# First tile of a token mixer: its input projection taken row block by row block, with the loads put in another order

## The chip, the cores and the metric

The kernel runs on one core of one Trainium2 chip. The metric is device time in microseconds (us) of that core; lower is better. Before the change, three runs took 5826.6, 5829.93 and 5834.68 us (median 5829.93).

## The reference, cut to what matters

Two transformer blocks follow one another on 2048 tokens of width 1024. The change lies in the opening of the first block, in its mixer:

```
hn   = rms_norm(x, norm_mix_w)            # x: 2048 x 1024
proj = hn @ w_in                          # w_in: 1024 x 2560 -> q, k, v, g, u (512 columns each)
q, k = rope(q, positions), rope(k, positions)
ret  = silu(g) * retention(q, k, v, ret_gn_w)
pool = pool_mixer(u, pool_w, pool_scale)
h    = x + concat([ret, pool]) @ w_out    # w_out: 1024 x 1024
```

After that come the router and 32 experts, a gated side branch, and the second block (latent attention, a bidirectional state-space layer, an output projection). None of these is touched.

## The kernel before, in words

The program is a row of phases, each of which waits for the one before. The first, `mixer_phase`, walks over 16 tiles of 128 tokens. Each engine has its own program, written out by hand in the order in which it runs, and engines meet at semaphores (`then_inc` and `wait_ge`); nothing reorders this. TensorE's program for a tile is `body` (L653): it transposes the x of the next tile, projects the next tile's five blocks of 512 columns between the steps of the present tile, and ends with the router's logits. `project(t, n)` (L630 to L638) makes one block of 512 columns: eight matmuls, one for each block of 128 rows of `w_in`, summed in one bank of PSUM, `PJ0` or `PJ1` in turn. ScalarE copies a bank out (`evacuate`, L319), times the row's 1/rms.

The first tile has no tile before it, so what it needs is made ahead of the loop, and this is where the change is:

- SyncE issues the loads in this order (L229 to L245): five small vectors and the broadcast `gain_moe` with `pos_i` (the positions) last, x of tile 0, zeros for the list of tokens `tok_list`, the eight row blocks of `w_in` (1280 KB each), the router's and pool's weights, eight row blocks of `w_out`, x of tile 1.
- ScalarE multiplies each row block of `w_in` in place by its gain (`scale_w_in`, L374): four blocks, then the tables (sin, cos, decays, L387 to L393), then the other four. Only the last block raises `w_in_scaled` (L397).
- VectorE makes angles and window matrices (L413 to L433, which ends with `dve_setup`), then, when `w_out` has landed, multiplies it by its gain (L551), and only then starts the rotation of tile 0 (L477).
- TensorE transposes x of tile 0 (L627), waits for `w_in_scaled`, makes the five projections one after another, 40 matmuls, waits for `dve_setup` to reach 2 (the scaled `w_out`), and goes into `body(0)`.
- GpSimd zeroes half of `xT` first (`zero_i`, L271), the source of the zeros that are stored to `tok_list`; ScalarE may overwrite `xT` only when that store has landed (L379).

Of the kernel before, what the change touches and what calls it, by code (L numbers as in the profile page):

```python
# [38 lines left out]
E, TOPK, CAP = 32, 4, SEQ  # L39
# [63 lines left out]
def mixer_phase(nc, I, S):  # L103
# [3 lines left out]
    with ExitStack() as ctx:  # L107
# [26 lines left out]
        pos_i = sb("pos_i", [P, TILES], I32)  # L134
# [9 lines left out]
        xT = sb("xT", [P, KD, P])  # L144
# [27 lines left out]
        zero_i = xT[:, 0:4, :].rearrange("p k c -> p (k c)").bitcast(I32)  # L172
# [30 lines left out]
        KV = pb("KV", BANK)  # L203
        Y = pb("Y", BANK)

        names = [f"w_in_rows{k}" for k in range(KD)] + """loads weights w_in_scaled pool_chain dve_setup act_setup pool_setup tables_in sines
# [18 lines left out]
        def _(sp):  # L225
            def load_x(t, par):
                sp.dma_start(x_sb[:, par, :], x_t[bass.ds(t, 1)].squeeze(0)).then_inc(s["x_loaded"], 16)

            sp.dma_start(gain_mix[:, :], I["norm_mix_w"][0].rearrange("(k p) -> p k", p=P)).then_inc(s["loads"], 16)  # L229
# [4 lines left out]
            sp.dma_start(pos_i[:, :], I["positions"][0].rearrange("(t p) -> p t", p=P)).then_inc(s["loads"], 16)  # L234
            load_x(0, 0)
            sp.wait_ge(s["pool_setup"], 1)
            sp.dma_start(S["tok_list"].rearrange("(p n) o -> p (n o)", p=P), zero_i[:, :]).then_inc(s["list_zeroed"], 16)
            for k in range(KD):
                sp.dma_start(w_in[:, k, :], I["w_in"][0, k * P:(k + 1) * P, :]).then_inc(s[f"w_in_rows{k}"], 16)
# [5 lines left out]
            load_x(1, 1)  # L245

# [22 lines left out]
        def _(pool):  # L269
            ch = Chain(pool, s["pool_chain"])  # L270
            ch.link(pool.memset(zero_i, 0))  # L271
            pool.sem_inc(s["pool_setup"], 1)
# [36 lines left out]
        def _(act):  # L309
# [9 lines left out]
            def evacuate(t, par, n, has_prev):  # L319
                act.wait_ge(s["proj_ps"], t * 5 + (n + 1))  # L320
                if n == 0:
                    act.wait_ge(s["rstd1_ready"], t + 1)
                if n == 4 and has_prev:
                    act.wait_ge(s["pl_ps"], t)
                if n < 2:
                    dst = qk[:, n * HEADS:(n + 1) * HEADS, :, :].rearrange("p h two f -> p (h two f)")
                else:
                    dst = vgu[:, par, (n - 2) * BANK:(n - 1) * BANK]
                act.activation(dst, PJ[n % 2][:, :], ACT.Copy, scale=rstd1[:, :]).then_inc(s["proj_sb"], 1)
# [44 lines left out]
            def scale_w_in(k):  # L374
                act.wait_ge(s[f"w_in_rows{k}"], 16)
                return act.activation(w_in[:, k, :], w_in[:, k, :], ACT.Copy, scale=gain_mix[:, k:k + 1])  # L376

            norm_x(0, 0)
            act.wait_ge(s["list_zeroed"], 16)  # L379
            copy_xT(0)  # L380

            act.wait_ge(s["loads"], 16 * 6)
            for k in range(4):
                scale_w_in(k)
            act.wait_ge(s["pool_setup"], 2)
# [9 lines left out]
            for k in range(4, KD):  # L395
                last = scale_w_in(k)
            last.then_inc(s["w_in_scaled"], 1)  # L397
            for n in range(5):
                evacuate(0, 0, n, False)
# [8 lines left out]
        def _(dve):  # L408
            ch = Chain(dve, s["dve_chain"])
            dve.wait_ge(s["pool_setup"], 2)  # L410
            dve.wait_ge(s["loads"], 16 * 6)
# [58 lines left out]
            def body(t, par, has_prev, has_next):  # L470
# [15 lines left out]
                if has_next:  # L486
                    norm_x(t + 1, True)
                dve.wait_ge(s["qkT_sb"], t + 1)
# [57 lines left out]

            norm_x(0, False)

            dve.wait_ge(s["weights"], 16 * (KD + 2))
            for k in range(KD):  # L550
                last = dve.tensor_scalar(w_out[:, k, :], w_out[:, k, :], gain_out[:, k:k + 1], None, ALU.mult)  # L551
            last.then_inc(s["dve_setup"], 1)
# [66 lines left out]
        def _(pe):  # L619
            pe.wait_ge(s["pool_setup"], 2)  # L620
# [32 lines left out]
            def body(t, par, has_prev, has_next):  # L653
# [58 lines left out]
                pe.wait_ge(s["mx_sb"], t + 1)  # L712
                project_out(0, range(4, KD))
# [22 lines left out]
            pe.wait_ge(s["w_in_scaled"], 1)  # L736
            for n in range(5):
                project(0, n, False)
            pe.wait_ge(s["dve_setup"], 2)
# [2283 lines left out]
```

## Time and profile before

| | us |
|---|---|
| median of three runs | 5829.93 (5826.6 to 5834.68) |
| the profiled execution | 5826.38 |
| its span, first to last instruction | 5824.6 |
| TensorE busy | 5316.9 (91%) |
| VectorE busy | 3248.5 (56%) |
| ScalarE busy | 2129.4 (37%) |
| GpSimd busy | 707.8 (12%) |

The span is what the profiler sees; the time of that execution is 1.8 us more. The mean granted clock of TensorE over the span is 0.962 of full speed. Of 40 slices of 145.6 us, the first has TensorE busy in six tenths; the next six are at nine tenths, and so is most of the rest. The last piece of the first phase ends about 1120 us into the span.

How the rows further on are read. A row of the timeline gives the start, the length, the engine, the line of the kernel, the operation, what it writes `<-` what it reads, the shape, how many records in a row were joined, and in brackets how long the engine had been idle before it and what released it. An fp32 matmul leaves two records (passes), so 40 matmuls are x80. The groups come in the order in which the prediction uses them.

### The profile page before, as it was taken

The page shows a single profiled execution, that of the slowest core. Times are in us where ns is not written, and L with a number is a line of the kernel's source. Part 1 is how long each engine was busy: PE and PEld are TensorE (multiplying, and loading weights), DVE is VectorE, ACT ScalarE, POOL GpSimd, SP SyncE. Part 2 cuts the span into 40 slices and gives each one's busy share as a digit, 9 for nine tenths or more (in the row PEclk, how much of TensorE's full clock was granted, in tenths as well). Part 3 has the DMA queues.
Part 4 walks back from the last instruction along what each step waited for, and adds up shares of the span by engine and source line. Part 5 has one row for each costly group of instructions (what it writes and reads, how often), then busy time and mean ns, then how long its engine had stood idle before and what let it go on. Part 6 is the DMA issues. An engine that isn't in the chain of part 4 may idle for free. (4 is left out here: it accounts for less than half of the span.)

```text
span 5824.6 us, 77622 instructions
## 1 busy us (share of the span) xinstructions
PE 5316.9 (91%) x24587; PEld 3508.7 (60%) x24922; DVE 3248.5 (56%) x6128; ACT 2129.4 (37%) x3190; POOL 707.8 (12%) x901
## 2 busy tenths in 40 slices
PE   6999999499999999999999999599995599999688
PEld 3555555366666666666666666355554477777365
DVE  3433433477676767777777777433335544443277
ACT  3111111144443545555555554222222433333243
POOL 0000000100000000000000000001003399100000
PEclk9999999699999999999999999799997799999899
DMA  3111211356464647777777676422322300000433
GB/s 136 57 50 54 72 50 50 115 176 192 159 207 150 211 152 238 237 237 240 239 232 234 229 227 204 161 93 103 103 89 97 82 5 8 6 6 6 170 108 101
DMA packets 424599, 769.80 MB, mean 132 GB/s; under 512 B 57440, under 2 KB 142368, under 8 KB 422816
## 3 DMA queue, kind: packets, MB, share of 16 engines
q1 hardware_dynamic: 363984, 607.16, 31.5%
q10 hardware_dynamic: 33216, 87.05, 4.9%
q0 software_dynamic: 27280, 74.02, 4.0%
q8 instruction: 73, 1.20, 0.1%
q14 instruction: 46, 0.38, 0.0%
HBM read 628.36 MB, written 139.76 MB: 132 GB/s over the span
## 5 line engine op out<-in xcount | busy, mean ns | idle before, releaser
L1070 DVE TENSOR_TENSOR w_lo<-stage,w_hi 128x1024 bf16<-128x1024 f32 (+1 forms) x800 | 929.6, 1178 | 201.3 <-ACT w_hi L939 142.3
L939 ACT ACTIVATE w_hi<-stage 128x1024 fp32r<-128x1024 f32 (+1 forms) x800 | 791.7, 1017 | 575.9 <-PE GU L773 291.2
L770 PE MATMUL GU<-w_hi,x_hl 128*128 128x512 f32 x2048 | 860.1, 420 | 19.0 <-DVE x_hl L1075 7.6
L771 PE MATMUL GU<-w_hi,x_hl 128*128 128x512 f32 x2048 | 811.6, 396 | 0.0
L636 PE MATMUL PJ<-w_in_sb,xT 128*128 128x512 f32 x1280 | 579.6, 607 | 41.9 <-ACT w_in_sb L376 31.5
L773 PE MATMUL GU<-w_lo,x_bf 128*128 128x512 bf16 x1920 | 480.6, 381 | 7.7
L770 PEld LDWEIGHTS GU<-w_hi,x_hl 128*128 128x128 f32 x2048 | 386.5, 189 | 135.1 <-issue 27.9
L770 PE MATMUL Y<-w_hi,a_hl 128*128 128x512 f32 x1024 | 456.8, 446 | 0.0
L636 PEld LDWEIGHTS PJ<-w_in_sb,xT 128*128 128x128 f32 x1280 | 244.2, 195 | 332.8 <-issue 286.2
L771 PEld LDWEIGHTS GU<-w_hi,x_hl 128*128 128x128 f32 x2048 | 387.5, 189 | 82.9
L771 PE MATMUL Y<-w_hi,a_hl 128*128 128x512 f32 x1024 | 404.4, 395 | 0.0
L773 PEld LDWEIGHTS GU<-w_lo,x_bf 128*128 128x128 bf16 x2048 | 174.7, 98 | 255.4 <-issue 89.8
L2337 DVE TENSOR_REDUCE ntop<-SC 128x1 f32<-128x2048 f32 x64 | 146.7, 2292 | 284.9 <-PE SC L2446 284.9
L900 POOL DMA_INDIRECT rows<-hn,ids x77 | 79.8, 1036 | 1780.4 <-PE TX L1209 1260.4
L2473 PE MATMUL O<-probsT,z_c 128*128 128x128 f32 x2048 | 276.1, 282 | 12.2 <-ACT probsT L2245 12.2
L945 ACT ACTIVATE acted<-pre 128x256 f32<-128x256 f32 (+1 forms) x304 | 131.9, 434 | 412.9 <-DVE pre L1098 399.8
L773 PE MATMUL Y<-w_lo,a_bf 128*128 128x512 bf16 x960 | 273.3, 383 | 4.4
L2473 PEld LDWEIGHTS O<-probsT,z_c 128*128 128x128 f32 x2048 | 248.2, 191 | 29.5 <-ACT probsT L2245 24.0
L1600 PE MATMUL G<-w_gate,hT 128*128 128x512 f32 x512 | 229.7, 608 | 30.4 <-ACT hT L1430 23.8
L1094 DVE TENSOR_TENSOR pre<-GU,b_gu 128x512 f32<-128x512 f32 x256 | 175.4, 685 | 137.1 <-PE GU L773 136.4
L643 PE MATMUL TR<-w_out_sb,catT 128*128 128x512 f32 x512 | 226.3, 595 | 0.7 <-ACT catT L358 0.7
L770 PEld LDWEIGHTS Y<-w_hi,a_hl 128*128 128x128 f32 x1024 | 193.2, 189 | 51.1
(537 smaller groups left out, 8752.2 us busy)
## 6 DMA issues: line engine op xcount, KB each, us to landing
stage<-in_expert_w_gate_up_dram SPq DMA_DIRECT2D x512, 512.0 KB, 5.2
stage<-in_expert_w_down_dram SPq DMA_DIRECT2D x224, 512.0 KB, 6.7
expert_rows<-zero_y SPq DMA_DIRECT2D x16, 2048.0 KB, 10.0
b_gu<-in_expert_b_gate_up_dram ACTq DMA_DIRECT2D x128, 256.0 KB, 4.9
expert_rows<-acted ACTq DMA_DIRECT2D x64, 512.0 KB, 2.9
b_d<-in_expert_b_down_dram ACTq DMA_DIRECT2D x32, 512.0 KB, 8.0
stage<-in_expert_w_down_dram SPq DMA_DIRECT2D x64, 256.0 KB, 3.3
z<-z_sb SPq DMA_DIRECT2D x16, 992.0 KB, 8.1
```

What stands on the lines that cost most here:

```text
L636: mm = pe.matmul(PJ[n % 2][:, :], xT[:, k, :], w_in[:, k, n * BANK:(n + 1) * BANK], start=(k == 0), stop=(k == KD - 1))
L643: mm = pe.matmul(TR[:, n * BANK:(n + 1) * BANK], catT[:, k, :], w_out[:, k, n * BANK:(n + 1) * BANK], start=(k == 4), stop=(k == 3))
L770: pe.matmul(out, high(k), w_high(k), start=(k == first), stop=False)
L771: pe.matmul(out, low(k), w_high(k), start=False, stop=False)
L773: mm = pe.matmul(out, short(k), w_low(k), start=False, stop=(k == last))
L939: act.activation(w_hi[:, c, ks, :], staged, ACT.Copy).then_inc(s["hi_done"], 1)
L945: act.activation(act_of(c)[0:n], gate[0:n], ACT.Tanh, scale=ALPHA / 2).then_inc(s["tanh_ready"], 1)
L1070: dve.tensor_tensor(w_lo[:, c, ks, :], staged, w_hi[:, c, ks, :], ALU.subtract).then_inc(s["lo_done"], 1)
L1094: ch.link(dve.tensor_tensor(pre[:, :], GU[c][:, :], b_gu[:, cols], ALU.add))
L1600: mm = pe.matmul(G[:, n * BANK:(n + 1) * BANK], hT[:, k, :], w_gate[:, k, n * BANK:(n + 1) * BANK], start=(k == 0), stop=(k == KD - 1))
L2337: dve.tensor_reduce(ntop[:, h % 2:h % 2 + 1], SC[:, :], AX, ALU.min).then_inc(s["max_done"], 1)
L2473: mm = pe.matmul(O[:, h * P:(h + 1) * P], c_rows(kt), probsT[:, j, kt % 4 * P:(kt % 4 + 1) * P], start=(kt == 0), stop=(kt == TILES - 1))
```

## The change

- SyncE: x of tile 0 is issued first, then `gain_mix` and `pos_i` (on a semaphore of their own, `gain_in`), then the eight row blocks of `w_in`, and the other small loads after them. The zeros for `tok_list` come last and are read from `zero_y`.
- GpSimd no longer zeroes `xT`; ScalarE no longer waits for that store.
- Each scaled row block of `w_in` raises `w_in_scaled`. For tile 0 TensorE loops over row blocks outside and the five column blocks inside, into five banks at once: `PJ0`, `PJ1`, `KV`, `Y` and the first half of `SC`.
- VectorE scales `w_out` in the body of tile 0, behind the rotation and the norm of tile 1; TensorE waits for it ahead of the first product with `w_out`.

```diff
+        first_banks = [PJ[0], PJ[1], KV, Y, SC]
...
-            sp.dma_start(gain_mix[:, :], I["norm_mix_w"][0].rearrange("(k p) -> p k", p=P)).then_inc(s["loads"], 16)
+            load_x(0, 0)
+            sp.dma_start(gain_mix[:, :], I["norm_mix_w"][0].rearrange("(k p) -> p k", p=P)).then_inc(s["gain_in"], 16)
+            sp.dma_start(pos_i[:, :], I["positions"][0].rearrange("(t p) -> p t", p=P)).then_inc(s["gain_in"], 16)
+            for k in range(KD):
+                sp.dma_start(w_in[:, k, :], I["w_in"][0, k * P:(k + 1) * P, :]).then_inc(s[f"w_in_rows{k}"], 16)
...
-            load_x(0, 0)
-            sp.wait_ge(s["pool_setup"], 1)
-            sp.dma_start(S["tok_list"].rearrange("(p n) o -> p (n o)", p=P), zero_i[:, :]).then_inc(s["list_zeroed"], 16)
-            for k in range(KD):
-                sp.dma_start(w_in[:, k, :], I["w_in"][0, k * P:(k + 1) * P, :]).then_inc(s[f"w_in_rows{k}"], 16)
...
             load_x(1, 1)
+            sp.wait_ge(s["pool_setup"], 1)
+            sp.dma_start(S["tok_list"].rearrange("(p n c) o -> p n (c o)", p=P, c=P),
+                         zero_y[:, :].bitcast(I32).unsqueeze(1).to_broadcast([P, E * CAP // (P * P), P])).then_inc(s["list_zeroed"], 16)
...
-            ch.link(pool.memset(zero_i, 0))
-            pool.sem_inc(s["pool_setup"], 1)
...
-                return act.activation(w_in[:, k, :], w_in[:, k, :], ACT.Copy, scale=gain_mix[:, k:k + 1])
+                act.activation(w_in[:, k, :], w_in[:, k, :], ACT.Copy, scale=gain_mix[:, k:k + 1]).then_inc(s["w_in_scaled"], 1)
...
-            act.wait_ge(s["list_zeroed"], 16)
...
-            act.wait_ge(s["loads"], 16 * 6)
+            act.wait_ge(s["gain_in"], 32)
...
-            dve.wait_ge(s["loads"], 16 * 6)
+            dve.wait_ge(s["gain_in"], 32)
...
+                if not has_prev:
+                    scale_w_out()
                 dve.wait_ge(s["qkT_sb"], t + 1)
...
+            def scale_w_out():
+                dve.wait_ge(s["loads"], 16 * 4)
+                dve.wait_ge(s["weights"], 16 * (KD + 2))
+                for k in range(KD):
+                    last = dve.tensor_scalar(w_out[:, k, :], w_out[:, k, :], gain_out[:, k:k + 1], None, ALU.mult)
+                last.then_inc(s["dve_setup"], 1)
...
                 pe.wait_ge(s["mx_sb"], t + 1)
+                if not has_prev:
+                    pe.wait_ge(s["dve_setup"], 2)
...
-            pe.wait_ge(s["w_in_scaled"], 1)
-            for n in range(5):
-                project(0, n, False)
-            pe.wait_ge(s["dve_setup"], 2)
+            for k in range(KD):
+                pe.wait_ge(s["w_in_scaled"], k + 1)
+                if k % 4 == 0:
+                    pe.wait_ge(s["xT_sb"], k // 4 + 1)
+                for n, bank in enumerate(first_banks):
+                    mm = pe.matmul(bank[:, 0:BANK], xT[:, k, :], w_in[:, k, n * BANK:(n + 1) * BANK],
+                                   start=(k == 0), stop=(k == KD - 1))
+                    if k == KD - 1:
+                        mm.then_inc(s["proj_ps"], 1)
```

TensorE at the opening of the program, before: the transposes of x of tile 0 into `TR`, then the projection of tile 0 into the two `PJ` banks.

```order
L627 MATMUL TR<-ident,x_sb 128x128 [waits x_loaded,pool_setup]
L627 MATMUL TR<-ident,x_sb 128x128 x7
L636 MATMUL PJ<-w_in_sb,xT 128x512 [waits xT_sb,w_in_scaled]
L636 MATMUL PJ<-w_in_sb,xT 128x512 x3
L636 MATMUL PJ<-w_in_sb,xT 128x512 [waits xT_sb]
L636 MATMUL PJ<-w_in_sb,xT 128x512 x11
L636 MATMUL PJ<-w_in_sb,xT 128x512 [waits proj_sb]
L636 MATMUL PJ<-w_in_sb,xT 128x512 x7
```

The same place after the change, with the first two of eight groups.

```order
L628 MATMUL TR<-ident,x_sb 128x128 [waits x_loaded,pool_setup]
L628 MATMUL TR<-ident,x_sb 128x128 x7
L744 MATMUL PJ<-w_in_sb,xT 128x512 [waits xT_sb,w_in_scaled]
L744 MATMUL PJ<-w_in_sb,xT 128x512
L744 MATMUL KV<-w_in_sb,xT 128x512
L744 MATMUL Y<-w_in_sb,xT 128x512
L744 MATMUL SC<-w_in_sb,xT 128x512
L744 MATMUL PJ<-w_in_sb,xT 128x512 [waits w_in_scaled]
L744 MATMUL PJ<-w_in_sb,xT 128x512
L744 MATMUL KV<-w_in_sb,xT 128x512
L744 MATMUL Y<-w_in_sb,xT 128x512
L744 MATMUL SC<-w_in_sb,xT 128x512
```

One wait ahead of 40 matmuls has become eight waits, each ahead of five matmuls; the waits for the evacuation of a bank in between are gone.

VectorE behind the set-up, before: the last step of 1/rms of tile 0, the scaling of `w_out`, the rotation of tile 0 (its first steps are shown).

```order
L81 SCALAR_TENSOR_TENSOR rstd<-nt,rstd 128x1 [waits dve_chain]
L551 TENSOR_SCALAR w_out_sb<-w_out_sb,gain_out 128x1024 [waits weights]
L551 TENSOR_SCALAR w_out_sb<-w_out_sb,gain_out 128x1024 x7
L477 TENSOR_TENSOR rope_a<-qk,cos 128x512 [waits proj_sb]
L478 TENSOR_TENSOR rope_b<-qk,sin 128x512
```

After the change, the end of the norm of tile 1 in the body of tile 0, and what follows it.

```order
L81 SCALAR_TENSOR_TENSOR rstd<-nt,rstd 128x1 [waits dve_chain]
L550 TENSOR_SCALAR w_out_sb<-w_out_sb,gain_out 128x1024 [waits weights,loads]
L550 TENSOR_SCALAR w_out_sb<-w_out_sb,gain_out 128x1024 x7
L488 TENSOR_TENSOR qxT<-qT,xi 128x512 [waits qkT_sb]
L492 TENSOR_TENSOR sT<-TR,decay 128x1024 [waits sc_ps]
```

The eight scalings stand behind the rotation now, ahead of the product of q with `xi`.

## Rows read from the trace of the kernel before

**Rows 1.** The timeline of TensorE up to 150 us.
```profile
10.58 1.94 PE L627 MATMUL TR<-ident,x_sb 128*128 128x128 f32 x8 [10.58 <-DMA x_sb<-in_x_dram]
44.04 36.45 PE L636 MATMUL PJ<-w_in_sb,xT 128*128 128x512 f32 x80 [31.52 <-ACT w_in_sb L376]
```

**Rows 2.** The timeline of ScalarE up to 150 us.
```profile
23.51 2.43 ACT L376 ACTIVATE w_in_sb<-w_in_sb,gain_mix 128x2560 f32<-128x2560 f32 x1 [0.66 <-DMA w_in_sb<-in_w_in_dram]
25.94 1.28 ACT L387 ACT_TABLE_LOAD   x1
...
34.60 9.38 ACT L376 ACTIVATE w_in_sb<-w_in_sb,gain_mix 128x2560 f32<-128x2560 f32 x4
53.06 0.69 ACT L329 ACTIVATE qk<-PJ,rstd 128x512 f32<-128x512 f32 x1 [9.08 <-PE PJ L636]
59.93 0.69 ACT L329 ACTIVATE qk<-PJ,rstd 128x512 f32<-128x512 f32 x1 [6.18 <-PE PJ L636]
...
80.53 0.69 ACT L329 ACTIVATE vgu<-PJ,rstd 128x512 f32<-128x512 f32 x1 [6.18 <-PE PJ L636]
```

**Rows 3.** The timeline of VectorE up to 150 us.
```profile
8.03 0.17 DVE L413 CAST pos_f<-pos_i 128x16 f32<-128x16 int32 x1 [7.90 <-DMA pos_i<-in_positions_dram]
...
25.18 0.23 DVE L433 TENSOR_SCALAR rel<-rel 128x128 f32<-128x128 f32 x1
...
48.52 5.39 DVE L551 TENSOR_SCALAR w_out_sb<-w_out_sb,gain_out 128x1024 f32<-128x1024 f32 x8 [10.10 <-DMA w_out_sb<-in_w_out_dram]
81.25 0.69 DVE L477 TENSOR_TENSOR rope_a<-qk,cos 128x512 f32<-128x512 f32 x1 [27.34 <-ACT vgu L329]
...
88.07 0.16 DVE L81 SCALAR_TENSOR_TENSOR rstd<-nt,rstd 128x1 f32<-128x1 f32 x1
91.27 0.69 DVE L489 TENSOR_TENSOR qxT<-qT,xi 128x512 f32<-128x512 f32 x1 [3.04 <-ACT kT L347]
```

**Rows 4.** The timeline of GpSimd up to 150 us.
```profile
0.90 0.53 POOL L271 MEMSET xT<- 128x512 int32 x1 [0.29 <-POOLq L3013]
...
6.80 0.14 POOL L287 IOTA tok_id<- 128x16 int32 x1
```

**Rows 5.** The timeline of SyncE's DMA queue up to 150 us.
```profile
3.60 0.43 SPq L234 DMA_DIRECT2D pos_i<-in_positions_dram  x1
...
7.30 4.07 SPq L239 DMA_DIRECT2D w_in_sb<-in_w_in_dram  x8
...
37.63 0.43 SPq L227 DMA_DIRECT2D x_sb<-in_x_dram  x1
```

**Rows 6.** Loads of x, then of w_in, up to 60 us, from issue to landing.
```profile
DMA to landing us min/median/max: 6.4/9.2/12.1
DMA to landing us min/median/max: 6.9/15.8/25.2
```

**Rows 7.** The timeline of TensorE in the body of tile 0 and at two tile boundaries.
```profile
105.87 0.38 PE L689 MATMUL SC<-band_prev,vgu 128*128 128x128 f32 x2
...
142.81 1.47 PE L627 MATMUL TR<-ident,x_sb 128*128 128x128 f32 x8
144.96 9.72 PE L636 MATMUL PJ<-w_in_sb,xT 128*128 128x512 f32 x16 [0.69 <-ACT xT L316]
...
208.65 1.09 PE L627 MATMUL TR<-ident,x_sb 128*128 128x128 f32 x8
...
271.62 1.09 PE L627 MATMUL TR<-ident,x_sb 128*128 128x128 f32 x8
```

**Rows 8.** Windows: stretch, length, busy of PE, PEld, DVE, ACT, POOL, clock, DMA.
```profile
144.00:148.00 4.00, 3.31 (x6) 1.49 (x5) 3.86 (x8) 2.40 (x6) 0.00 (x0) 0.50 1.13 343
...
912.00:916.00 4.00, 3.31 (x10) 2.00 (x9) 3.76 (x13) 2.39 (x6) 0.00 (x0) 0.50 1.13 344
...
1064.00:1068.00 4.00, 2.15 (x6) 0.61 (x4) 3.52 (x15) 0.00 (x0) 0.00 (x0) 1.00 0.00 0
1068.00:1072.00 4.00, 3.53 (x8) 2.05 (x9) 0.41 (x1) 0.60 (x1) 0.00 (x0) 0.57 0.00 0
```

More of the change, by code:

```diff
@@ L171, in mixer_phase @@
         hnT = xT
-        zero_i = xT[:, 0:4, :].rearrange("p k c -> p (k c)").bitcast(I32)
         lg = sb("lg", [P, E])
@@ L204, in mixer_phase @@
         Y = pb("Y", BANK)
-        names = [f"w_in_rows{k}" for k in range(KD)] + """loads weights w_in_scaled pool_chain dve_setup act_setup pool_setup tables_in sines
+        first_banks = [PJ[0], PJ[1], KV, Y, SC]
+        names = [f"w_in_rows{k}" for k in range(KD)] + """loads gain_in weights w_in_scaled pool_chain dve_setup act_setup pool_setup tables_in sines
             x_loaded xT_ps xT_sb sumsq1 rstd1_ready proj_ps proj_sb rope_done qk_ps qkT_sb qx_sb sc_ps kv_ps
@@ L233, in _ @@
             sp.dma_start(bias_rt[:, :], row(I["router_b"][0])).then_inc(s["loads"], 16)
-            sp.dma_start(pos_i[:, :], I["positions"][0].rearrange("(t p) -> p t", p=P)).then_inc(s["loads"], 16)
-            load_x(0, 0)
-            sp.wait_ge(s["pool_setup"], 1)
-            sp.dma_start(S["tok_list"].rearrange("(p n) o -> p (n o)", p=P), zero_i[:, :]).then_inc(s["list_zeroed"], 16)
-            for k in range(KD):
-                sp.dma_start(w_in[:, k, :], I["w_in"][0, k * P:(k + 1) * P, :]).then_inc(s[f"w_in_rows{k}"], 16)
             sp.dma_start(w_rt[:, :, :], I["router_w"][0].rearrange("(k p) e -> p k e", p=P)).then_inc(s["weights"], 16)
@@ L317, in copy_xT, with evacuate @@
                 act.activation(xT[:, 4:8, :], TR[:, BANK:], ACT.Copy).then_inc(s["xT_sb"], 1)
-            def evacuate(t, par, n, has_prev):
+            def evacuate(t, par, n, has_prev, bank=None):
                 act.wait_ge(s["proj_ps"], t * 5 + (n + 1))
@@ L328, in evacuate @@
                     dst = vgu[:, par, (n - 2) * BANK:(n - 1) * BANK]
-                act.activation(dst, PJ[n % 2][:, :], ACT.Copy, scale=rstd1[:, :]).then_inc(s["proj_sb"], 1)
+                act.activation(dst, (bank or PJ[n % 2])[:, 0:BANK], ACT.Copy, scale=rstd1[:, :]).then_inc(s["proj_sb"], 1)
             def weigh(t):
@@ L375, in scale_w_in @@
                 act.wait_ge(s[f"w_in_rows{k}"], 16)
-                return act.activation(w_in[:, k, :], w_in[:, k, :], ACT.Copy, scale=gain_mix[:, k:k + 1])
+                act.activation(w_in[:, k, :], w_in[:, k, :], ACT.Copy, scale=gain_mix[:, k:k + 1]).then_inc(s["w_in_scaled"], 1)
             norm_x(0, 0)
-            act.wait_ge(s["list_zeroed"], 16)
             copy_xT(0)
-            act.wait_ge(s["loads"], 16 * 6)
+            act.wait_ge(s["gain_in"], 32)
             for k in range(4):
                 scale_w_in(k)
-            act.wait_ge(s["pool_setup"], 2)
+            act.wait_ge(s["pool_setup"], 1)
             act.wait_ge(s["dve_setup"], 1)
@@ L395, in _ @@
             for k in range(4, KD):
-                last = scale_w_in(k)
-            last.then_inc(s["w_in_scaled"], 1)
+                scale_w_in(k)
             for n in range(5):
-                evacuate(0, 0, n, False)
+                evacuate(0, 0, n, False, first_banks[n])
             body(0, 0, False, True)
@@ L409, in _ @@
             ch = Chain(dve, s["dve_chain"])
-            dve.wait_ge(s["pool_setup"], 2)
-            dve.wait_ge(s["loads"], 16 * 6)
+            dve.wait_ge(s["pool_setup"], 1)
+            dve.wait_ge(s["gain_in"], 32)
             ch.link(dve.tensor_copy(pos_f[:, :], pos_i[:, :]))
@@ L545, in body @@
                                   ALU.add).then_inc(s["mask_done"], 1)
+            def scale_w_out():
[4 more added lines that the diff above has]
+                last.then_inc(s["dve_setup"], 1)
             norm_x(0, False)
[L549 to L552, printed above, removed]
             body(0, 0, False, True)
@@ L619, in _ @@
         def _(pe):
-            pe.wait_ge(s["pool_setup"], 2)
+            pe.wait_ge(s["pool_setup"], 1)
             def transpose_x(t, par, has_prev):
```

## The prediction

> **What bounds the kernel now.** I read the timeline of each engine over the first 150 us, then the landing times of the loads, then the windows with TensorE's clock at the places where the clock changes level. The slices of the page say why there: TensorE is busy in nine tenths or more of most slices, but in six tenths of the first. The first tile's opening is the hole.
>
> In that hole TensorE transposes x of tile 0 at 10.58 us, idles 31.52 us until ScalarE has scaled the last row block of `w_in`, and runs the 40 matmuls of the projection from 44.04 for 36.45 us [rows 1]. ScalarE is busy through it. It scales four row blocks as they land, the last of them until 25.94, makes the tables, and scales the other four in one piece from 34.60 to 43.98 [rows 2]. It then has five banks to copy out, the last from 80.53 [rows 2]. VectorE made its set-up from 8.03 to 25.41, scaled `w_out` from 48.52 to 53.91 and waited 27.34 us for the fifth bank before the rotation could start at 81.25 [rows 3]. So the order of events is one chain: positions land, VectorE's set-up, tables, four scalings, 40 matmuls, rotation. Everything behind runs at TensorE's pace.
>
> **The chain after the change, step by step.** All times are of the profiled execution (5826.38 us, 3.55 us below the median of the runs shown).
>
> 1. VectorE's start. It needs the positions and GpSimd's set-up. The positions were issued at 3.60 and used at 8.03, 4.43 us later [rows 3, 5]. Now they are third in the queue, not sixth. The issues ahead of them take about 0.5 us each, so they go out near 1.9 and should be there near 6.3, if the 512 KB of x ahead of them do not hold them up. GpSimd's last index row starts at 6.80 and ends at 6.94, and loses at least the 0.53 us of zeroing [rows 4]: 6.4. Bounds are 6.4 and, if the positions come no sooner than before, 8.03. I take 6.7.
> 2. Set-up: 25.41 - 8.03 = 17.38 us [rows 3], unchanged, so it ends at 24.1. ScalarE's first four scalings do not delay the tables: x is first in the queue now and `w_in` follows it, so ScalarE should be through at about 21. Before, row block 0 was issued at 7.30 and landed 6.9 us later at the earliest [rows 5, 6]; now it is issued near 2.4 with less ahead of it, and I put its landing at 9 to 10, ready scaled at 12.0, and the others 3.1 us apart. This term has slack of three microseconds, and costs nothing while it has it. TensorE's transposes and ScalarE's copies of xT come at about 6.5 to 9.6 and are no part of the chain either.
> 3. Tables: from the table load at 25.94 to the fifth scaling at 34.60 is 8.66 us [rows 2]. In both orders the load waits for VectorE, so the fifth scaling starts at 24.1 + 8.7 = 32.8 and ends, at 2.43 us for one [rows 2], at 35.2.
> 4. Matmuls. One matmul at full pace is a fifth of a row block, and 6.87 us (from 53.06 to 59.93) for eight is 0.859 us [rows 2], so a row block of five takes 4.3 us. The first four blocks start at 12.0 and need 17.2 us, plus the slow start: before, the first eight matmuls took 53.06 - 44.04 = 9.02 us where later ones took 6.87, 2.15 us more [rows 1, 2]. They end near 31.3, under the tables, and that is half of the projection gone from the chain. The second four blocks start at 35.2. ScalarE delivers one per 2.34 us and TensorE uses one per 4.3, so TensorE runs without a gap until 35.2 + 17.2 = 52.4.
> 5. The clock in the gap. TensorE now idles some 3.9 us between blocks 3 and 4. In a place with less idling the clock fell: TensorE was busy 2.15 of 4 us at 1064 us with the full clock, and the next window stands at 0.57 of it, near the lower level (1.2 GHz, where full is 2.4) for most of it [rows 8]. Bounds are no loss and 3.4 us (one fall as at tile 1, where two windows, of 4 us each, hold the low level in full or in part, at half pace). The slow start of 2.15 is the nearest row, and I take 1.6. The last matmul then ends at 54.0.
> 6. The copying out: five banks finish 0.86 us apart and a copy takes 0.69 [rows 2], so only the last is behind the last matmul, as before. The rotation starts at about 54.8 and not 81.25.
>
> The sum: 80.5 - 54.0 = 26.5 us from tile 0. By the bounds: 28.1 with an early start and no fall, 23.4 with 8.03 and 3.4.
>
> **What is moved behind this.** VectorE's 5.39 us for `w_out` go from an idle stretch to one between the norm of tile 1 (last step at 88.07) and the product with `xi` at 91.27, which had waited 3.04 us [rows 3]. The product starts at 88.2 + 5.4 = 93.7 in old time, 2.4 us later. Nothing is queued on VectorE that TensorE wants before then, and TensorE wants the product first at 105.87 [rows 7]. So it costs nothing, with 11 us of cover. If that cover failed (if `w_out` landed late), each microsecond past it would cost one. The wait for the scaled `w_out` is at the first product with it, later still.
>
> x of tile 1 is the next thing that TensorE needs, and this is the load to watch. It was issued at 37.63 and landed 12.1 us later, at 49.7 [rows 5, 6], with 30 us to spare. Now it is wanted at 54. The loads run one behind the other at the pace of the DMA engines, so what counts is what lies ahead: the row blocks start some 4.8 us sooner, the 512 KB of `gain_moe` and the small vectors have moved between them and x of tile 1, and the 256 KB of zeros have left. That puts the landing near 47, seven microseconds early. Bounds: 44.9 and 49.7, both before 54; the term is nothing. The zeros of `tok_list` go last on SyncE's queue, ahead of the store of h, which waits for the end of tile 0 anyway, and are needed by GpSimd only after tile 1. That, too, is nothing.
>
> From the rotation on, the instructions are the same up to these waits, and no load of a later phase is issued before the first phase has ended, so the 26.5 us should reach the end. What does not carry over exactly is the clock. At 14 boundaries between tiles TensorE does short work with gaps, and at six of them the granted clock drops to 0.50 for a few microseconds (the first and the last full window are shown [rows 8]). The tile with such a drop took 208.65 - 142.81 = 65.84 us, and the one without 271.62 - 208.65 = 62.97, so a drop costs 2.87 us [rows 7]. Which boundaries get one will change when everything is 26 us earlier. I count no gain or loss, and give or take two drops, 6 us.
>
> **The time.** 5826.38 - 26.5 = 5799.9 for an execution like the profiled one, and 5829.93 - 26.5 = 5803.4 from the median. I say 5801.
>
> **The rivals.**
>
> - The matmuls in row order run slow. Five accumulations are open at once and the bank changes with every matmul. For: these matmuls come behind gaps, which is where this trace shows the clock fall [rows 8]. Against: the loads of xT and the moving rows per matmul are the same, the trace has no row of slow matmuls in a dense stretch, and blocks 4 to 7 are dense. At half pace throughout (the first half, started at 12, then ends at 46.4, past 35.2), the projection takes 68.7 us from 12.0 and ends at 80.7: no gain. With only the second half slow, that half takes 34.4 us and the last matmul ends at 69.6: a gain of 10.9, or 5819. The page "TensorE: Matmul & The Clock Gate" of the Trainium skill, in "A second HAM failure mode: psum-queue depth-cycling", tells of a kernel whose cycling through banks left small idle times between its matmuls, so that the clock went back and forth. No run here shows such a thing, and by it the time would be that of this rival. Chance 6%.
> - A load comes late. If the queue does not move up as I reckon and x of tile 1 lands at 66, TensorE stands for 12 us, and the gain is 14.5: 5815. For: the margin shrinks from 30 us to about 7. Against: even with no shift at all it lands at 49.7 [rows 5, 6]. Chance 5%.
> - The clock takes it back. If all 14 boundaries draw a drop and not six, that is 8 times 2.87 = 23 us, which leaves 3.5 us of gain: 5826. Against: drops came at one place in two or three whatever the tile. Chance 4%.
> - The other side: TensorE, fed in bits from 12 us on, does not come to its full clock at the opening and stays at the low level through the body of tile 0. At half pace the projection ends at 69.6 and the body, 62.3 us from 80.53 to 142.81 [rows 2, 7], takes up to twice that: a loss of 62.3 against a gain of 10.9, slower by 51, at 5881. It decides against the change from about 11 us lost in the body on, or 22 us of it at half pace. For: the low level stood at tile boundaries in spite of work in three quarters or more of the window [rows 8]. Against: every such stretch there ended within 8 us once the matmuls were dense. Chance 3%.
> - That the change does not do what it says: no idle time of TensorE would go. The eight waits are in the program, and row blocks 0 to 3 were scaled at 25.94 [rows 2], so at least half of the matmuls must move. Chance 1%.
>
> **How the numbers follow.** The forecast has 81%. Its own range is 5792 to 5812: 23.4 to 28.1 us of gain, two drops more or less, and the 8 us by which the runs before differ among themselves. The rivals that gain less lie at its upper edge; I give 5790 to 5814. What this measurement can tell from no change is about 0.2%, 11.7 us, so faster means below 5818. The forecast and the late load are faster (86%), the first rival by half (3%): 0.89. The same: half of the first, the third and the last: 0.08. Slower: 0.03.
>
> **What would show it right or wrong.** TensorE's timeline should show bursts of ten records from 12 us, then a gap until 35, then 40 records in one piece until 52 to 56, and the transposes of x of tile 1 right behind them, released by nothing. If they wait for a load, the second rival holds. VectorE's set-up should start at 6.4 to 7 and end 17.4 us later; if not, step 1 fails. Records of a pass at 0.85 us apart beyond the first 4 us and the gap speak for the first rival. The rotation starts at 53 to 57. The stretch from there to the end of the first phase should be as long as before but for multiples of 2.9 us; if it is longer by 10 or more, the gain was given back there. The forecast is wrong if the rotation of tile 0 starts after 60, or if phases behind the first differ by over 5 us.

## The result, and the profile after

| | before | after |
|---|---|---|
| median, first comparison (5 runs each) | 5829.93 (5826.6 to 5837.22) | 5800.64 (5794.96 to 5804.71) |
| the profiled execution | 5826.38 | 5800.64 |
| its span | 5824.6 | 5798.6 |
| mean granted clock | 0.962 | 0.961 |

The changed kernel is faster by half a per cent: ratio 0.9947, 95% interval 0.9936 to 0.9958, which is 29 us by the medians and 25.7 us between the two profiled executions. The forecast was 5801. A second group of runs of the same two kernels on one chip gave 5798.19 against 5828.15, ratio 0.9954 (0.9941 to 0.9967). One run stood out among all those that are used here: a run of rows_only took 5856.98 us at a mean granted clock of 0.938, where every other had 0.960 to 0.964.

TensorE's timeline after the change, up to 150 us. It answers to [rows 1].

```profile
6.32 1.97 PE L628 MATMUL TR<-ident,x_sb 128*128 128x128 f32 x8 [6.32 <-POOL tok_id L286]
14.49 3.78 PE L744 MATMUL PJ<-w_in_sb,xT 128*128 128x512 f32 x4 [6.20 <-ACT w_in_sb L375]
18.06 1.56 PE L744 MATMUL KV<-w_in_sb,xT 128*128 128x512 f32 x2
...
33.19 1.02 PE L744 MATMUL SC<-w_in_sb,xT 128*128 128x512 f32 x2
34.97 1.98 PE L744 MATMUL PJ<-w_in_sb,xT 128*128 128x512 f32 x4 [0.76 <-ACT w_in_sb L375]
...
51.38 1.02 PE L744 MATMUL SC<-w_in_sb,xT 128*128 128x512 f32 x2
52.24 1.04 PE L628 MATMUL TR<-ident,x_sb 128*128 128x128 f32 x8
54.05 7.11 PE L637 MATMUL PJ<-w_in_sb,xT 128*128 128x512 f32 x16 [0.78 <-ACT xT L315]
```

Where there were 31.52 us of idle time and then 80 records in one piece, there is now idle time of 6.20 us, 40 records from 14.49, a pause of 0.76 us, and 40 records more until the transposes of tile 1 at 52.24. Before, those started at 80.33, behind the projection.

ScalarE after the change, answering to [rows 2]: the first scaling, the fourth, the tables, the last four scalings in one piece, and the five copies.

```profile
12.01 2.43 ACT L375 ACTIVATE w_in_sb<-w_in_sb,gain_mix 128x2560 f32<-128x2560 f32 x1 [2.60 <-DMA w_in_sb<-in_w_in_dram]
...
21.18 2.43 ACT L375 ACTIVATE w_in_sb<-w_in_sb,gain_mix 128x2560 f32<-128x2560 f32 x1 [0.67 <-DMA w_in_sb<-in_w_in_dram]
23.82 1.28 ACT L385 ACT_TABLE_LOAD   x1 [0.22 <-DVE rel L430]
...
32.49 9.39 ACT L375 ACTIVATE w_in_sb<-w_in_sb,gain_mix 128x2560 f32<-128x2560 f32 x4
49.01 0.69 ACT L328 ACTIVATE qk<-PJ,rstd 128x512 f32<-128x512 f32 x1 [7.13 <-PE PJ L744]
...
52.44 0.69 ACT L328 ACTIVATE vgu<-SC,rstd 128x512 f32<-128x512 f32 x1 [0.17 <-PE SC L744]
```

The table load now waits 0.22 us for VectorE, so after the change the chain goes through VectorE's set-up, but narrowly: the fourth scaling had ended at 23.61. Before, it was the other way round. VectorE's set-up had ended at 25.41 [rows 3], and the table load started at 25.94, right behind the fourth scaling [rows 2], which had waited for its row block to land. VectorE, answering to [rows 3]:

```profile
6.37 0.17 DVE L410 CAST pos_f<-pos_i 128x16 f32<-128x16 int32 x1 [6.24 <-POOL tok_id L286]
...
53.16 0.69 DVE L474 TENSOR_TENSOR rope_a<-qk,cos 128x512 f32<-128x512 f32 x1 [16.85 <-ACT vgu L328]
...
60.08 5.39 DVE L550 TENSOR_SCALAR w_out_sb<-w_out_sb,gain_out 128x1024 f32<-128x1024 f32 x8
65.38 0.68 DVE L488 TENSOR_TENSOR qxT<-qT,xi 128x512 f32<-128x512 f32 x1
```

It starts at 6.37, released by GpSimd and no longer by the positions. The rotation starts at 53.16 where it started at 81.25 [rows 3]: 28.1 us sooner. The scaling of `w_out` stands behind it and nothing on TensorE waits for it.

x of tile 1 is the load with the least to spare. Its issue on SyncE's queue, and the summary of the two loads of x up to 60 us (the maximum is this one):

```profile
38.05 0.64 SPq L227 DMA_DIRECT2D x_sb<-in_x_dram  x1
DMA to landing us min/median/max: 3.7/8.0/12.3
```

### The profile page after: what moved, and what is told of

Read it like the earlier page. It is cut to its first block and busy times, and to the rows that moved or that the text cites. A ratio compares the mean times of both kernels' runs of the same rounds, so it can differ in the third digit from the quotient of the medians.

```text
span 5798.6 us, 77622 instructions
## 1 busy us (share of the span) xinstructions
PE 5317.6 (92%) x24587; PEld 3510.1 (61%) x24922; DVE 3250.4 (56%) x6128; ACT 2129.6 (37%) x3190; POOL 707.6 (12%) x900
## 5 line engine op out<-in xcount | busy, mean ns | idle before, releaser
L637 PE MATMUL PJ<-w_in_sb,xT 128*128 128x512 f32 x1200 | 540.6, 604 | 10.4 <-ACT xT L315 10.4
L778 PEld LDWEIGHTS GU<-w_hi,x_hl 128*128 128x128 f32 x2048 | 386.5, 189 | 134.5 <-issue 28.1
L637 PEld LDWEIGHTS PJ<-w_in_sb,xT 128*128 128x128 f32 x1200 | 227.4, 194 | 279.4 <-issue 264.8
L2481 PEld LDWEIGHTS O<-probsT,z_c 128*128 128x128 f32 x2048 | 248.2, 191 | 29.5 <-ACT probsT L2253 24.0
```

What stands on the lines that cost most here:

```text
L637: mm = pe.matmul(PJ[n % 2][:, :], xT[:, k, :], w_in[:, k, n * BANK:(n + 1) * BANK], start=(k == 0), stop=(k == KD - 1))
L778: pe.matmul(out, high(k), w_high(k), start=(k == first), stop=False)
L2481: mm = pe.matmul(O[:, h * P:(h + 1) * P], c_rows(kt), probsT[:, j, kt % 4 * P:(kt % 4 + 1) * P], start=(kt == 0), stop=(kt == TILES - 1))
```

## The experiments

The first four ran as one group, the last three as another. All of them are edits of the changed kernel. The times that say most are those inside the trace; the times of whole runs scatter by 10 us and more. Each row of the table is one execution; the two of the changed kernel agree within 0.06 us in the first two columns.

| kernel | rotation of tile 0 starts | transposes of q, k start | x of tile 2 to x of tile 15 | profiled execution |
|---|---|---|---|---|
| before | 81.25 | 89.08 | 834.5 | 5826.38 |
| changed | 53.16 | 61.00 | 833.2 | 5800.64 |
| changed, again | 53.11 | 60.94 | 833.3 | 5797.03 |
| rows_only | 54.57 | 62.40 | 836.4 | 5809.29 |
| loads_only | 79.37 | 87.21 | 838.3 | 5827.73 |
| w_out_early | 53.06 | 60.90 | 833.5 | 5796.49 |
| tables_longer | 58.17 | 66.00 | 834.5 | 5802.61 |
| x1_late | 53.09 | 68.08 | 833.8 | 5807.4 |
| gain_in_x | 49.30 | 56.43 | 840.7 | 5804.21 |

The fourth column is the difference between the starts of TensorE's transposes of tile 2 and of tile 15, 13 tiles whose instructions are the same in all of these kernels.

### The load order undone: rows_only

```diff
-            load_x(0, 0)
             sp.dma_start(gain_mix[:, :], I["norm_mix_w"][0].rearrange("(k p) -> p k", p=P)).then_inc(s["gain_in"], 16)
-            sp.dma_start(pos_i[:, :], I["positions"][0].rearrange("(t p) -> p t", p=P)).then_inc(s["gain_in"], 16)
-            for k in range(KD):
-                sp.dma_start(w_in[:, k, :], I["w_in"][0, k * P:(k + 1) * P, :]).then_inc(s[f"w_in_rows{k}"], 16)
...
             sp.dma_start(bias_rt[:, :], row(I["router_b"][0])).then_inc(s["loads"], 16)
+            sp.dma_start(pos_i[:, :], I["positions"][0].rearrange("(t p) -> p t", p=P)).then_inc(s["gain_in"], 16)
+            load_x(0, 0)
+            for k in range(KD):
+                sp.dma_start(w_in[:, k, :], I["w_in"][0, k * P:(k + 1) * P, :]).then_inc(s[f"w_in_rows{k}"], 16)
```

> The changed kernel with its loads in the order of before (small vectors, positions, x of tile 0, w_in), the row order of tile 0 kept. My theory: nearly all of the gain is the row order, the load order only moves VectorE's set-up and with it the chain by 1.6 us. VectorE starts near 8.0, the fifth row block is ready near 36.6, the last of the 40 matmuls ends near 54.0 and the rotation starts near 54.8 (changed kernel: 53.16). Time about 5802 to 5804, ratio to before 0.995. Rival (the loads are half of it, since they fill the DMA engines earlier): rotation after 60, time above 5812.

Measured: 5804.48 us (median of 12, or 5803.82 without the run of 5856.98; before 5826.52, median of 23), ratio 0.9966 (0.995 to 0.9982). VectorE started at 7.78, the fifth row block went to TensorE at 36.38, and the rotation started at 54.57.

```profile
36.38 1.98 PE L744 MATMUL PJ<-w_in_sb,xT 128*128 128x512 f32 x4 [0.93 <-ACT w_in_sb L375]
53.65 1.04 PE L628 MATMUL TR<-ident,x_sb 128*128 128x128 f32 x8
```

The pause ahead of the fifth block is 0.93 us, released by ScalarE, and the piece behind it is as long as in the changed kernel (53.65 - 36.38 = 17.27). The table load waits for VectorE here too (0.35 us), so the whole chain is later by as much as VectorE's start (7.78 against 6.37). The load order is worth 1.4 us of the 28.1, as the first theory said; it had put 1.6. GpSimd's missing memset and the late zeros of `tok_list` are still in this kernel; they were not undone by themselves.

### The row order undone: loads_only

```diff
-            for k in range(KD):
-                pe.wait_ge(s["w_in_scaled"], k + 1)
...
-                for n, bank in enumerate(first_banks):
+            pe.wait_ge(s["w_in_scaled"], KD)
+            pe.wait_ge(s["xT_sb"], 2)
+            for n, bank in enumerate(first_banks):
+                for k in range(KD):
```

> The changed kernel with the 40 matmuls of tile 0 column block by column block again, behind the eighth scaled row block; loads, five banks and the place of the w_out scaling as changed. My theory: the matmuls start near 41.9 and end near 78.3, the rotation starts near 79.1, 2.1 us sooner than before (81.25); time 5828, ratio 0.9996 to before, not to be told from no change. Rival: a gain of 10 us or more from the loads alone.

Measured: 5825.34 us (median of 11; before 5826.52), ratio 1.0001 (0.9992 to 1.001). The matmuls started at 41.87 and the rotation at 79.37, 1.9 us sooner than before.

```profile
41.87 16.14 PE L743 MATMUL PJ<-w_in_sb,xT 128*128 128x512 f32 x32 [33.59 <-ACT w_in_sb L375]
78.45 1.04 PE L628 MATMUL TR<-ident,x_sb 128*128 128x128 f32 x8
```

Its ScalarE shows the old pace of the column blocks, here the first two copies:

```profile
51.18 0.69 ACT L328 ACTIVATE qk<-PJ,rstd 128x512 f32<-128x512 f32 x1 [9.37 <-PE PJ L743]
58.05 0.69 ACT L328 ACTIVATE qk<-PJ,rstd 128x512 f32<-128x512 f32 x1 [6.18 <-PE PJ L743]
```

Taken from before, this kernel gives 1.9 us at the rotation and rows_only 26.7; together they give 28.1. The parts add up to 0.5 us more than the whole. Both kernels keep the zeros of `tok_list` at the end of the queue, so what that gives is counted twice: in rows_only, with the other loads in the order of before, the last four scalings start at 33.89 where they started at 34.60 [rows 2].

Against the changed kernel the row order is worth 26.2 us, and that has two parts. The last 20 matmuls wait for the fifth scaled row block and not the eighth: 34.97 against 41.87, 6.9 us. And 20 matmuls, with the slow start of the engine, are done before that: behind the wait stand 17.27 us of work and not 36.58 (41.87 to the transposes of tile 1 at 78.45), 19.3 us.

The pace of single matmuls answers the first rival. With column order, eight matmuls take 6.87 us between two copies, 0.859 each, also in these five banks. In row order 20 of them take 52.24 - 34.97 = 17.27 us, 0.864 each. So the change of bank with every matmul costs next to nothing (0.1 us over the 20), and the first rival's price is not there. The rule of the Trainium skill that I had set beside that rival ("TensorE: Matmul & The Clock Gate", "A second HAM failure mode: psum-queue depth-cycling") tells of a kernel in which cycling through banks left small idle times between groups of matmuls and the clock went back and forth. In this case the matmuls of either half followed one another without idle time, and the granted clock read 1.00 in every window of 4 us from 16 to 56 us; the rule's condition did not come up, so this trace does not test it.

### The place of the w_out scaling undone: w_out_early

```diff
                 if has_next:
                     norm_x(t + 1, True)
-                if not has_prev:
-                    scale_w_out()
...
             norm_x(0, False)
+            scale_w_out()
             body(0, 0, False, True)
```

> The changed kernel with the scaling of w_out ahead of the rotation, as before. w_out lands near 48 and the scaling takes 5.39 us, so by my theory the rotation is put off by only about 1 us (start 53.2 to 54.5), and TensorE, which is in the first projection of tile 1 until 61, does not notice: the transposes of q and k still start near 61.0 and the later body is the same; the place of the scaling is worth nothing. Rival (it is needed): the transposes start at 62 or later with an idle time before them released by VectorE.

Measured: 5796.49 us (one run). Rotation at 53.06, transposes of q and k at 60.90, both as in the changed kernel.

```profile
47.48 5.39 DVE L548 TENSOR_SCALAR w_out_sb<-w_out_sb,gain_out 128x1024 f32<-128x1024 f32 x8 [11.27 <-DMA w_out_sb<-in_w_out_dram]
53.06 0.69 DVE L474 TENSOR_TENSOR rope_a<-qk,cos 128x512 f32<-128x512 f32 x1 [0.19 <-ACT vgu L328]
```

The scaling ended near 52.87 (47.48 + 5.39) and the rotation still waited 0.19 us for ScalarE. I had expected it to be put off by about 1 us; it was not put off at all. Where it stands makes no difference here, but only just: a rotation any earlier would have met it.

### More work between the tables and the fifth scaling: tables_longer

```diff
             last.then_inc(s["act_setup"], 1)
+            flat = ang[:, :, :].rearrange("p t f -> p (t f)")
+            for out in (catT[:, 0:4, :].rearrange("p k c -> p (k c)"), catT[:, 4:8, :].rearrange("p k c -> p (k c)"),
+                        pooledT[:, :, :].rearrange("p k c -> p (k c)"), tanh_g[:, :], hn_sb[:, 0:BANK], hn_sb[:, BANK:],
+                        yc[:, :, :].rearrange("p h e -> p (h e)")):
+                act.activation(out, flat, ACT.Exp)
             for k in range(4, KD):
```

> The changed kernel with seven more 128x512 Exp on ScalarE between the tables and the fifth scaling (some 3.8 us), written to buffers that are not in use yet. It tells whether the chain runs through the tables and what a gap of TensorE costs. My theory: fifth scaling at 36.3, TensorE idles 4.5 us ahead of row block 4 where the changed kernel idled 0.76, rotation 3.8 us later (57.0) if the clock stays, and 5.1 to 6 us later (58.3 to 59.2) if it falls, as I had assumed it would for a gap of 3.9 us; I expect the fall. Rival (the chain runs elsewhere, through the loads): the rotation moves by less than 2 us.

Measured: 5802.61 us (one run). The last four scalings started at 36.05 (changed: 32.49) and the rotation at 58.17, 5.0 us later. TensorE:

```profile
38.51 3.44 PE L749 MATMUL PJ<-w_in_sb,xT 128*128 128x512 f32 x4 [5.36 <-ACT w_in_sb L375]
...
57.25 1.04 PE L633 MATMUL TR<-ident,x_sb 128*128 128x128 f32 x8
```

and its windows, with the clock in the third column from the end:

```profile
32.00:36.00 4.00, 1.16 (x3) 0.19 (x1) 3.11 (x13) 3.96 (x9) 0.00 (x0) 1.00 1.06 297
36.00:40.00 4.00, 1.49 (x2) 0.83 (x3) 0.18 (x2) 4.00 (x3) 0.00 (x0) 0.76 0.95 326
40.00:44.00 4.00, 4.00 (x9) 1.66 (x8) 0.00 (x0) 4.00 (x3) 0.00 (x0) 0.81 1.02 413
```

Of the 5.0 us, 3.54 are the later start of the fifth block (38.51 against 34.97). The other 1.47 are in the length of the second half (57.25 - 38.51 = 18.74 against 17.27): the first four records took 3.44 us where they took 1.98, at a granted clock of 0.76 and 0.81 of full, so part of these windows was at 1.2 GHz. This shows two things: the chain does run through the tables, nearly one for one, and a clock that falls in a pause costs 1.5 us here. The pause was 5.36 us and not the 4.5 expected, because the first half had ended 1.1 us sooner than in the changed kernel's first trace (33.15 against 34.21): its first row block was scaled from 11.42, not 12.01, and its slow start was shorter.

### The load of x of tile 1 put off: x1_late

```diff
             sp.wait_ge(s["x_loaded"], 16)
+            sp.wait_ge(s["proj_ps"], 5)
             load_x(1, 1)
```

> The changed kernel with the load of x of tile 1 issued only when the fifth bank is done (52.2). In the changed kernel that load landed at 50.4 and TensorE used it at 52.24, with 1.8 us to spare where 5 were forecast. The theory that this load is the next limit says: it lands near 56, TensorE's transposes of tile 1 wait for it, and everything from there is 3.5 to 4 us later (first projection of tile 1 at 57.5 to 58), while the rotation stays at 53.2. Rival (the wait is made up for, since TensorE stands for VectorE's rotation anyway): the transposes of q and k start within 1 us of 61.0.

Measured: 5807.4 us (one run). The load was issued at 52.42 and landed 3.9 us later, at 56.3.

```profile
56.34 1.74 PE L629 MATMUL TR<-ident,x_sb 128*128 128x128 f32 x8 [4.01 <-DMA x_sb<-in_x_dram]
58.86 9.39 PE L638 MATMUL PJ<-w_in_sb,xT 128*128 128x512 f32 x16 [0.78 <-ACT xT L316]
68.08 1.04 PE L665 MATMUL SC<-ident,rot 128*128 128x128 f32 x8
```

The load is the next limit, as the theory said, and nothing behind makes up for it. But the size was wrong: the projection of tile 1 started 4.8 us later and the transposes of q and k 7.1 us later, where I had put 3.5 to 4. The wait itself is 4.01 us; the rest is the clock. The window from 56 to 60 us had 0.58 of it:

```profile
56.00:60.00 4.00, 2.88 (x10) 2.00 (x11) 1.82 (x3) 1.89 (x3) 0.00 (x0) 0.58 0.05 17
60.00:64.00 4.00, 4.00 (x7) 1.68 (x6) 3.35 (x15) 0.23 (x2) 0.00 (x0) 0.57 0.00 0
```

The transposes took 1.74 us and not 1.04, and 16 records 9.39 and not 7.11. These two differences are 2.98 us.

### The gain folded into x: gain_in_x

```diff
+            sp.wait_ge(s["x_loaded"], 16)
+            load_x(1, 1)
...
-                act.wait_ge(s[f"w_in_rows{k}"], 16)
+                act.wait_ge(s["rows_used"], k + 1)
...
-            copy_xT(0)
...
-            for k in range(4):
-                scale_w_in(k)
+            for k in range(KD):
+                act.activation(xT[:, k, :], TR[:, k * P:(k + 1) * P], ACT.Copy, scale=gain_mix[:, k:k + 1]).then_inc(s["xT_sb"], 1) if k % 4 == 3 else act.activation(xT[:, k, :], TR[:, k * P:(k + 1) * P], ACT.Copy, scale=gain_mix[:, k:k + 1])
+            scale_w_in(0)
...
-            for k in range(4, KD):
+            for k in (1, 2, 3, 4):
                 scale_w_in(k)
...
+            for k in (5, 6, 7):
+                dve.wait_ge(s["rows_used"], k + 1) if k < 7 else dve.wait_ge(s["proj_ps"], 5)
+                dve.tensor_scalar(w_in[:, k, :], w_in[:, k, :], gain_mix[:, k:k + 1], None, ALU.mult).then_inc(s["w_in_by_dve"], 1)
...
+                    if not has_prev:
+                        pe.wait_ge(s["w_in_scaled"], 5)
+                        pe.wait_ge(s["w_in_by_dve"], 3)
...
-                pe.wait_ge(s["w_in_scaled"], k + 1)
+                pe.wait_ge(s[f"w_in_rows{k}"], 16)
...
+                    elif n == 4:
+                        mm.then_inc(s["rows_used"], 1)
```

> For tile 0 the gain of the norm goes into the copies of xT (eight ScalarE copies with a scale instead of two), so TensorE takes each row block of w_in as it lands, unscaled; the blocks are scaled behind their last use (five by ScalarE, three by VectorE), and x of tile 1 is loaded right behind w_in. By the theory that the scaled blocks and the tables are the chain of the changed kernel, TensorE starts near 12 (changed: 14.49), runs without a gap to 48.5, and the first projection of tile 1 starts near 50.3 (changed: 54.05), 3.8 us sooner: time some 4 us below the changed kernel, hardly to be told by the times. Rival (something else, the third scaling on VectorE or the load of x of tile 1, takes its place): the projection of tile 1 starts no sooner than 53.

Measured: 5797.69 us (median of 5; before 5828.15), ratio 0.9945 (0.9932 to 0.9958); the changed kernel beside it had 5798.19.

```profile
11.72 3.45 PE L750 MATMUL PJ<-w_in_sb,xT 128*128 128x512 f32 x4 [3.46 <-DMA w_in_sb<-in_w_in_dram]
47.63 1.04 PE L631 MATMUL TR<-ident,x_sb 128*128 128x128 f32 x8
49.49 7.11 PE L640 MATMUL PJ<-w_in_sb,xT 128*128 128x512 f32 x16 [0.82 <-DVE w_in_sb L556]
```

Inside the trace the step did what was forecast: TensorE ran from 11.72 without a pause, and the first projection of tile 1 started at 49.49, 4.6 us sooner than in the changed kernel, where 3.8 had been put. The rival's place is named in the last row, VectorE's third scaling, but it charges almost nothing: the wait is 0.82 us where ScalarE's copy of `xT` took 0.78. x of tile 1 was issued at 9.21 and landed 25.5 us later, at 34.7, with 12.9 us to spare and not 1.9. In the whole time it cannot be told: the two intervals lie on one another. In the profiled execution the 13 tiles behind it took 840.7 us and not 833.2, more than all of the gain. It is a version that starts sooner and is not shown to be faster.

### The changed kernel once more: after_again

No edit.

> The changed kernel unaltered, on the same chip as the others of this group, for its time beside gain_in_x and for a second trace. Expected 5797 to 5804, 26 to 30 us below before. By the theory that what differs between the early gain (28.1 us at the rotation) and the gain at the end is the clock's falls at tile boundaries, the early part repeats within 0.5 us (rotation at 53.2) and the boundaries that fall are others.

Measured: 5798.19 us (median of 6; before 5828.15), ratio 0.9954 (0.9941 to 0.9967). The rotation started at 53.11, 0.05 us from the first trace. At the boundary to tile 2 the clock dropped in the first trace (0.50 from 116 to 120 us) and did not in this one. First the changed kernel's first trace, then this one:

```profile
114.75 1.97 PE L628 MATMUL TR<-ident,x_sb 128*128 128x128 f32 x8
117.40 9.17 PE L637 MATMUL PJ<-w_in_sb,xT 128*128 128x512 f32 x16 [0.69 <-ACT xT L315]
```

```profile
114.65 1.09 PE L628 MATMUL TR<-ident,x_sb 128*128 128x128 f32 x8
116.43 7.13 PE L637 MATMUL PJ<-w_in_sb,xT 128*128 128x512 f32 x16 [0.69 <-ACT xT L315]
```

The same instructions at the same place, a tenth of a microsecond apart in time, take 2.9 us more in one execution than in the other. From the transposes of one tile to those of the next, five of the 13 took 64.6 us or more in either trace and the others 63.2 or less, but not the same five: tiles 2, 4, 9, 10 and 12 in the first, 6, 8, 11, 13 and 14 in the second. So which boundaries fall is not fixed by the kernel.

## Why the prediction was right

**The chain after the change was the right one.** VectorE's set-up, tables, four scalings, matmuls, rotation: tables_longer moved a link in the middle of it by 3.56 us, and the fifth block went to TensorE 3.54 us later. Undoing the row order took 26.2 us of the 28.1 away (53.16 to 79.37), undoing the load order 1.4, and undoing the third part nothing. No other wait took the place of the one removed.

For the kernel before, the chain had one link wrong. I wrote that in both orders the table load waits for VectorE. It stood behind the fourth scaling, 0.53 us after VectorE was done (25.94 against 25.41), and so hung on the landing of the fourth row block. This left the sum alone, since it started from VectorE's new time, but it means that the two branches ran side by side within half a microsecond.

**Step by step.** VectorE's start was put at 6.7 and came at 6.37, at its lower bound, since GpSimd (6.26) and no longer the positions (1.83 + 4.4 = 6.2) came last. The fifth block was put at 35.2 and came at 34.97. The pace of 4.3 us for a row block held to 0.01, but for the one behind the pause (4.39). The projection's end was put at 54.0 and came at 52.4, and the gain from tile 0 at 26.5 and came at 28.1. That is the figure I gave as the bound for an early start and no fall of the clock, but the bound was added up wrong: without the 1.6 of the clock the gain is 28.1 at a start of 6.7, and 28.4 at one of 6.4. The measured gain lies between the forecast and the true bound.

**The number itself was luck.** 5801 and 5800.64 agree far better than the terms do. The gain at the rotation was put 1.6 us too small, the five runs differ by 10 us among themselves, and the second group of the same kernel gave 5798.19.

**Where a step was off.** Step 2 put the landing of the first row block at 9 to 10 us and its scaled form at 12.0; the scaling only started at 12.01, and TensorE started at 14.49. The first half of the matmuls thus ended near 34.2 and not 31.3. ScalarE was through with the first four at 23.61 and not at about 21, so of the three microseconds of slack that the step claimed 0.14 were left before VectorE was done (23.52 + 0.23). This cost nothing, because all of it fell into waits that were there anyway. And because the late start of the first half filled that pause, step 5 failed: the pause was not 3.9 us but 0.76, and the clock, for which I had counted 1.6 us, did not fall. Where a pause of that kind was made, the fall cost 1.47 us (tables_longer, 5.36 us of pause) or 2.98 us (x1_late, 4.01 us), both inside the bounds of none to 3.4, so the 1.6 can't be called right either; what was wrong was that there would be a fall. The two misses were one miss, and its sign was in my favor by luck. The bursts of ten records that I had named as a sign did not show either: from 14.49 the 40 records ran in one piece, as the step's own figures say they must, with a block every 3.1 us and 4.3 us to use one.

**What was moved.** The product with `xi` started at 65.38, at once behind the `w_out` scaling, and TensorE's wait for it, ahead of the matmuls at 77.79, took no time. The cover was 11.7 us. For x of tile 1 the margin was less than said. The load was issued at 38.05, later than before, and landed 12.3 us after that, at 50.4, not near 47. TensorE wanted it at 52.24: 1.9 us to spare, not seven. The first row block was issued 4.8 us sooner (2.45 against 7.30) but landed only 2.3 us sooner: at 11.95, against 14.2 before, and not at 9 to 10. Right ahead of it now stand `gain_mix` and the positions, 12 KB that go as single words of 4 bytes. From 4 to 6 us the DMA engines took 2847 packets, 2841 of them under 512 bytes, and moved 0.07 MB; from 8 to 12 us they took 178 packets and moved 1.66 MB. That these two small loads held the row blocks up is how I read it; no run took them away. The second rival was right about the place and only lacked two microseconds. x1_late shows what it would have charged: 7.1 us for a load 5.9 us later.

**From the rotation to the end.** The two profiled executions differ by 28.1 us at the rotation and by 25.7 at the end. ScalarE's first scaling of an expert's weights starts at 1130.4 and 1101.4, 29.0 us apart; the attention's first row maximum at 4655.6 and 4629.6, 26.0 apart; the output stage's first normalized tile at 5559.1 and 5530.5, 28.6 apart; its last at 5818.9 and 5792.9, 26.0 apart. The difference goes down and up again. A cost of the change would be there each time the kernel runs, and it is not: in after_again the same four places stand at 1101.2, 4626.1, 5529.3 and 5789.3, which is 29.2, 29.5, 29.8 and 29.6 us sooner than before. So in that execution all of the early gain reached the end, and what comes and goes in the first one belongs to it and not to the change. I take it for the clock, as forecast. That is shown for one tile boundary by the pair of rows above; for the later phases it is not shown.

**The other rivals.** That the clock takes the gain back at all boundaries did not come: the 13 tiles took 833 to 841 us in nine traces. Every trace had tiles with the drop and tiles without. The one on the other side, TensorE staying at the low level through tile 0, did not come either: from the rotation to the transposes of tile 2 the changed kernel took 61.6 us, as before (61.56).

## What to carry to other kernels

Where an engine waits for the last of several pieces and then works through all of them, look for a loop order that takes a piece at a time, and count how many accumulators it needs: here five free banks of PSUM put half of a 36 us projection beneath a wait (19.3 us) and let the other half start three scalings sooner (6.9 us). The order of the loads in front of it, which looked like part of the same matter, was worth 1.4 us. After such a change read the margin of the next load from the new trace: in x1_late an idle time of 4 us on TensorE put what follows off by 7.

A gain of 4.6 us that the trace shows plainly can vanish in a kernel whose executions differ by 10; then the start of a late instruction is the better measure, and the verdict on the whole stays open.

## What the runs showed of the hardware that was not expected

- TensorE's pace did not depend on the bank in this stage: 0.859 us for an fp32 128x128x512 matmul with eight in a row into one bank, 0.864 with a new bank for every one.
- Pauses of 0.76, 0.93, 1.36 (w_out_early) and 1.50 us ahead of the fifth row block (the last one in after_again, where the second half took 17.28 us) left the clock at full; those of 4.01 and 5.36 us were followed by windows at 0.57 to 0.81 of it. The cost behind the pause was 2.98 us after the one of 4.01 and 1.47 us after the one of 5.36: of these two, one execution each, the longer pause cost less.
- At the opening of the program the matmuls ran at half pace for about 4 us (four records in 3.78 us from 14.49, where 1.88 was usual later) while the granted clock in the windows read 1.00. That this was the low level of the clock is how I read the spacing of the records; the column does not show it.
- SyncE stood for long at the issue of loads much smaller than a row block, 8.33 us at the second `gain_out` (2 KB) and 11.11 us at `gain_moe` (512 KB), and before the change 20.90 us at `w_pool` (256 KB). It moved with the order of the loads: x of tile 1, the last one that TensorE needs in this stage, was issued between 36.58 and 38.24 us in all seven traces in which it stands at the end of the queue, and its landing moved by 0.7 us (49.7 to 50.4) with the change. That the queue was full is how I read it; no run tried it.
